# Rotary sums and the heads' high and low parts taken off DVE in the attention of an encoder trunk

## What is computed

```python
p = u @ w_in                                   # rq rk rv rg | dq dk dv
q = _rotary(rq, pos); k = _rotary(rk, pos) * 128 ** -0.5
# _rotary: concatenate([x1 * cos - x2 * sin, x1 * sin + x2 * cos])
ret = silu(rg) * groupnorm(retention(q, k, v)) # four heads "r"
a = softmax(q0 k0) - lam * softmax(q1 k1)      # four heads "d", q and k RMS-normed
dif = _rmsnorm(a @ v, subln_g) * (1.0 - lam_init)
h = h + jnp.concatenate([ret, dif], axis=-1) @ w_out
```

## Time and profile before

| | before |
|---|---|
| median of 3 runs | 1962.74 us (1961.9 to 1963.89) |
| the profiled execution, its own time | 1963.26 us |
| its span | 1960.6 us |
| PE busy | 1902.9 us (97%) |
| DVE busy | 1190.9 us (61%) |
| Pool busy | 1163.0 us (59%) |
| ACT busy | 915.5 us (47%) |
| granted PE clock, mean | 0.989 |

### The profile page before, as it was taken

How to read it: one execution, slowest core, us unless ns; L and a number is a source line. 1 busy time by engine, 2 the same in 40 slices (tenths; PEclk the granted TensorE clock), 3 DMA queues, 4 the chain that set the end, 5 groups by cost and what they waited for, 6 DMA issues and landing times.

```text
span 1960.6 us, 29609 instructions
## 1 busy us (share of the span) xinstructions
PE 1902.9 (97%) x11578; PEld 1692.3 (86%) x11578; DVE 1190.9 (61%) x1897; ACT 915.5 (47%) x1461; POOL 1163.0 (59%) x626
## 2 busy tenths in 40 slices
PE   7999999998899999999999999999988999999997
PEld 6989989886688998989879898998867889899896
DVE  7736667428665753736677376663385667457276
ACT  6534535446434643524565254454464355345254
POOL 4857757454243776857458585755533347588582
PEclk9999999999899999999999999999998999999999
DMA  3333423231122331332234233223211132323231
GB/s 130 133 108 109 137 94 108 75 107 55 54 65 72 111 130 65 108 108 88 85 105 143 77 109 108 87 87 118 87 54 54 54 108 87 118 92 115 86 104 69
DMA packets 54999, 186.46 MB, mean 95 GB/s; under 512 B 6441, under 2 KB 7977, under 8 KB 54861
## 3 DMA queue, kind: packets, MB, share of 16 engines
q1 hardware_dynamic: 53136, 181.61, 28.0%
q10 hardware_dynamic: 1724, 2.96, 0.5%
HBM read 182.44 MB, written 3.15 MB: 95 GB/s over the span
## 4 chain that ended last, share of the span: by engine, by line
PE 77%; DVE 8%; POOL 5%; ACT 4%; issue 3%; DMA 1%; DVEq 0%; ACTq 0%; POOLq 0%
PE bank L661 16%; PE bank L663 16%; PE bank L662 16%; PE pair L661 8%; PE pair L662 8%; PE pair L663 8%; POOL w_lo L573 1%; DVE neg_max L1737 1%; ACT s L1318 1%; PE pair L934 1%; PE bank L949 1%; DVE bank L1428 1%; DVE s L1724 1%; POOL w_lo_x L592 0%; POOL w_lo L592 0%
## 5 line engine op out<-in xcount | busy, mean ns | idle before, releaser
L565 POOL TENSOR_TENSOR w_lo<-raw,w_hi 128x1024 fp32r<-128x1024 f32 (+1 forms) x124 | 293.5, 2373 | 458.4 <-ACT w_hi L1016 458.4
L661 PE MATMUL bank<-hg_hi,w_hi 128*128 128x256 f32 (+1 forms) x1400 | 449.3, 321 | 2.3 <-DVE bank L1444 2.3
L663 PE MATMUL bank<-hg_hi,w_lo 128*128 128x256 f32 (+1 forms) x1400 | 444.6, 318 | 0.0
L662 PE MATMUL bank<-hg_lo,w_hi 128*128 128x256 f32 (+1 forms) x1400 | 444.2, 317 | 0.0
L661 PEld LDWEIGHTS bank<-hg_hi,w_hi 128*128 128x128 f32 x1400 | 265.5, 190 | 25.1 <-issue 7.9
L662 PEld LDWEIGHTS bank<-hg_lo,w_hi 128*128 128x128 f32 x1400 | 265.4, 190 | 18.2 <-issue 1.2
L663 PEld LDWEIGHTS bank<-hg_hi,w_lo 128*128 128x128 f32 x1400 | 265.3, 190 | 17.9
L1016 ACT ACTIVATE w_hi<-raw 128x1024 fp32r<-128x1024 f32 (+1 forms) x124 | 128.3, 1036 | 263.6 <-PE bank L663 127.8
L1411 DVE SCALAR_TENSOR_TENSOR h<-pair,h 128x512 f32<-128x512 f32 x100 | 68.9, 690 | 246.1 <-PE pair L663 245.8
L661 PE MATMUL pair<-a_hi,w_hi 128*128 128x512 f32 x440 | 172.5, 392 | 1.9 <-issue 1.3
L663 PE MATMUL pair<-a_hi,w_lo 128*128 128x512 f32 x440 | 171.6, 390 | 0.0
(11 more groups left out here) (269 smaller groups left out, 4951.9 us busy)
## 6 DMA issues: line engine op xcount, KB each, us to landing
raw<-in_w_gu SPq DMA_DIRECT2D x96, 512.0 KB, 3.7
raw_x<-in_w_gu SPq DMA_DIRECT2D x80, 512.0 KB, 4.1
raw<-in_w_p SPq DMA_DIRECT2D x56, 512.0 KB, 3.5
raw_x<-in_w_dn SPq DMA_DIRECT2D x32, 512.0 KB, 3.8
raw<-in_w_dn SPq DMA_DIRECT2D x32, 512.0 KB, 4.0
raw<-in_w_o SPq DMA_DIRECT2D x16, 512.0 KB, 3.5
raw_x<-in_w_dn SPq DMA_DIRECT2D x16, 384.0 KB, 3.6
raw<-in_w_dn SPq DMA_DIRECT2D x16, 384.0 KB, 3.4
```

The costliest lines, as they stand in the source:

```text
L565: pool.tensor_tensor(columns(lo_), raw_tiles(RAW_AT["e", e], TILES_OF[e]), columns(hi).bitcast(F32), ALU.subtract).then_inc(lo_done, 1)
L661: pe.matmul(out, hi[:, 0, :], m_hi, start=first, stop=False)
L662: pe.matmul(out, hi[:, 0, :], m_lo, start=False, stop=False)
L663: return pe.matmul(out, lo_[:, 0, :], m_hi, start=False, stop=last)
```

## The change

The rotary sum goes from DVE to Pool: `rotate` waits for `proj_free`, which DVE signals after its third multiplication, and stands ahead of `lo` in the same step. The high part of a finished head goes to ACT and its low part to Pool, both in the step after the one in which DVE finished the head, ahead of the rest of Pool's step and right behind `split` on ACT. Two semaphores are new: `head_done` (DVE to ACT) and `head_hi` (ACT to Pool). In ACT's step the square of a "d" head's output and its high part now come before the wait for `mix_ready`. The loops of ACT and Pool have one more step. PE's program is not changed.

```diff
--- before.py
+++ after.py
@@ -129,6 +129,7 @@
 
 STEPS = 31
 N_ITEMS = HEADS * BATCHES
+SUB_LATER = 1
 
 
 def scores_at(n): return 11 + n
@@ -166,7 +167,7 @@
 
 H_UPDATES = KD * (2 * len(CHUNKS) + 1)
 STATS = 1 + 8 + HEADS + HEADS + 1 + 1
-DVE_STEPS = 72
+DVE_STEPS = 56
 
 EARLY = 6
 FIRST_X = 3
@@ -380,6 +381,8 @@
         ret_sq = signal("ret_sq", HEADS)
         o_ret_free = signal("o_ret_free", HEADS)
         ret_rms = signal("ret_rms", HEADS)
+        head_done = signal("head_done", KD)
+        head_hi = signal("head_hi", KD)
         mix_ready = signal("mix_ready", KD)
         log_exp = signal("log_exp", 2)
         log_done = signal("log_done", 2)
@@ -631,13 +634,31 @@
                 pool.wait_ge(sq_hi, at(sq_hi, l, n + 1))
                 pool.tensor_tensor(lo_, squares, hi.bitcast(F32), ALU.subtract).then_inc(sq_lo, 1)
 
+            def rotate(l, t):
+
+                kind, hd = TILES[t]
+                dst = rkq[:, hd % 2, int(kind == "rq"), :]
+                pool.wait_ge(proj_free, at(proj_free, l, t + 1))
+                pool.tensor_tensor(dst, dst, s3[:, 0, :], ALU.add).then_inc(rot_ready, 1)
+
+            def lo_head(l, which, out):
+                k = MIX_ORDER.index(which)
+                pool.wait_ge(head_hi, at(head_hi, l, k + 1))
+                pool.tensor_tensor(a_lo[:, k, :], out, a_hi[:, k, :].bitcast(F32), ALU.subtract).then_inc(mix_ready, 1)
+
             def attention(l):
                 for t in range(AHEAD):
                     lo(l, E_ATT + t)
-                for t in range(STEPS):
+                for t in range(STEPS + 1):
+                    if (hd_n := at_step(subln_at, HEADS, t - SUB_LATER)) is not None:
+                        lo_head(l, ("d", hd_n), o_d[:, :])
+                    if (hd_n := at_step(ret_var_at, HEADS, t - 1)) is not None:
+                        lo_head(l, ("r", hd_n), o_r[:, :])
                     if t < PROJ_TILES:
+                        kind, hd = TILES[t]
+                        if kind in ("rk", "rq"):
+                            rotate(l, t)
                         lo(l, E_ATT + AHEAD + t)
-                        kind, hd = TILES[t]
                         if kind in ("dk", "dq"):
                             lo_square(l, "qk", 2 * hd + (kind == "dq"))
                     if (n := at_step(mixv_at, N_ITEMS, t)) is not None and n % 2:
@@ -1272,13 +1293,22 @@
                         act.wait_ge(decay_arg, at(decay_arg, l, i + 1))
                         act.activation(decay[:, i, :], decay[:, i, :], ACT.Exp).then_inc(decay_exp, 1)
 
+            def hi_head(l, which, out):
+                k = MIX_ORDER.index(which)
+                act.wait_ge(head_done, at(head_done, l, k + 1))
+                act.activation(a_hi[:, k, :], out, ACT.Copy).then_inc(head_hi, 1)
+
             def attention(l):
                 factor(l, stat_index("mix"), rms[:, :], 1.0, rms_ready)
-                for t in range(STEPS):
+                for t in range(STEPS + 1):
                     kind, hd = TILES[t] if t < PROJ_TILES else (None, 0)
                     if t < PROJ_TILES:
                         act.wait_ge(proj_done, at(proj_done, l, t + 1))
                         split(l, E_ATT + AHEAD + t)
+                    if (hd_n := at_step(subln_at, HEADS, t - SUB_LATER)) is not None:
+                        hi_head(l, ("d", hd_n), o_d[:, :])
+                    if (hd_n := at_step(ret_var_at, HEADS, t - 1)) is not None:
+                        hi_head(l, ("r", hd_n), o_r[:, :])
                     if kind == "rg":
                         act.wait_ge(proj_free, at(proj_free, l, t + 1))
                         act.activation(rg[:, hd, :], rg[:, hd, :], ACT.Silu).then_inc(rg_ready, 1)
@@ -1305,12 +1335,12 @@
                     if (n := at_step(mixv_at, N_ITEMS, t)) is not None and n % 2:
                         hd_n = n // 2
                         act.wait_ge(mixv_done, at(mixv_done, l, n + 1))
+                        act.activation(s3[:, 1, :], o_diff, ACT.Square).then_inc(o_d_sq, 1)
+                        hi_square(l, "sub", hd_n, o_d_sq)
                         if hd_n:
 
                             act.wait_ge(mix_ready, at(mix_ready, l, MIX_ORDER.index(("d", hd_n - 1)) + 1))
-                        act.activation(s3[:, 1, :], o_diff, ACT.Square).then_inc(o_d_sq, 1)
                         act.activation(o_d[:, :], o_diff, ACT.Copy).then_inc(o_d_ready, 1)
-                        hi_square(l, "sub", hd_n, o_d_sq)
                     if (n := at_step(scores_at, N_ITEMS, t)) is not None:
                         act.wait_ge(max_ready, at(max_ready, l, n + 1))
                         for i in range(2 * QT):
@@ -1687,14 +1717,6 @@
                                              op0=ALU.subtract, op1=ALU.subtract).then_inc(dve_step, 1)
                     next_step(l)
 
-            def mixed(l, which, source):
-
-                k = MIX_ORDER.index(which)
-                dve.tensor_copy(a_hi[:, k, :], source).then_inc(dve_step, 1)
-                dve.wait_ge(dve_step, next_step(l))
-                dve.tensor_tensor(a_lo[:, k, :], source, a_hi[:, k, :].bitcast(F32), ALU.subtract)\
-                    .then_inc(mix_ready, 1)
-
             def attention(l):
                 dve.wait_ge(rms_ready, at(rms_ready, l, 2))
                 dve.wait_ge(bias_in, at(bias_in, 0, 48))
@@ -1752,9 +1774,7 @@
                     if (hd_n := at_step(subln_at, HEADS, t)) is not None:
                         dve.wait_ge(sub_rms, at(sub_rms, l, hd_n + 1))
                         dve.scalar_tensor_tensor(out=o_d[:, :], in0=o_d[:, :], scalar=SUB_GAIN, in1=sub_factor,
-                                                 op0=ALU.mult, op1=ALU.mult).then_inc(dve_step, 1)
-                        dve.wait_ge(dve_step, next_step(l))
-                        mixed(l, ("d", hd_n), o_d[:, :])
+                                                 op0=ALU.mult, op1=ALU.mult).then_inc(head_done, 1)
                     if (hd_n := at_step(ret_var_at, HEADS, t)) is not None:
                         if hd_n:
                             dve.wait_ge(mix_ready, at(mix_ready, l, MIX_ORDER.index(("r", hd_n - 1)) + 1))
@@ -1764,9 +1784,7 @@
                         dve.wait_ge(o_ret_free, at(o_ret_free, l, hd_n + 1))
                         if hd_n == 0:
                             dve.wait_ge(rg_ready, at(rg_ready, l, HEADS))
-                        dve.tensor_tensor(o_r[:, :], o_r[:, :], rg[:, hd_n, :], ALU.mult).then_inc(dve_step, 1)
-                        dve.wait_ge(dve_step, next_step(l))
-                        mixed(l, ("r", hd_n), o_r[:, :])
+                        dve.tensor_tensor(o_r[:, :], o_r[:, :], rg[:, hd_n, :], ALU.mult).then_inc(head_done, 1)
 
             def take_over(l, t):
 
@@ -1784,8 +1802,6 @@
 
                     dve.tensor_tensor(cross[0:HALF], source[HALF:P], cs[HALF:P, 1, :], ALU.mult)
                     dve.tensor_tensor(cross[HALF:P], source[0:HALF], cs[0:HALF, 1, :], ALU.mult).then_inc(proj_free, 1)
-                    dve.wait_ge(proj_free, at(proj_free, l, t + 1))
-                    dve.tensor_tensor(dst, dst, cross, ALU.add).then_inc(rot_ready, 1)
                     return
                 if kind in ("dk", "dq"):
                     if hd == 3:
```

## The result

| | before | changed |
|---|---|---|
| median, runs on the same chip | 1962.6 us (10 runs, 1960.23 to 1963.89) | 1967.59 us (10 runs, 1966.61 to 1968.03) |
| ratio, 95% interval | | 1.0025 (1.0015 to 1.0035) |
| the profiled execution: own time, span | 1963.26, 1960.6 us | 1967.66, 1964.8 us |
| DVE busy, Pool busy | 1190.9, 1163.0 us | 1166.0, 1198.6 us |

The changed kernel is 5.0 us slower (by the interval 2.9 to 6.9). DVE lost 25 us of work and Pool gained 36 us, and PE, which bounds the kernel, came out later.

A forecast was written before the change was run, and what follows sets the result against it. PE, 97% busy, was taken to bound the kernel. Terms of 0.1 + 2.4 + 1.1 + 1.35 = 4.95 us a layer, 9.9 for both, on 1963.26 gave 1973.2, stated as 1972; range 1953 to 1977.

The forecast's parts named there:

- The mechanism: DVE's softmax port instructions each wait out a running Pool instruction; Pool instructions standing ready back to back decide the delay.
- the walk through step 17: Ahead of stall D: Pool's low part, rotary sum, weights and squares in turn; softmax ready at 507.5, as before.
- Stall E not longer: Rival, chance 0.22: L1719 precedes d1's low part or one of Pool's four is not ready; +2.9, 1965.6 us.
- Faster: Rival, chance 0.20: Pool does not get back to back into the softmax; 1943.5, or 1952.5 with E alone gone.
- Slower still: Rival, chance 0.08: Pool's squares of steps 24 and 26 are late too; up to +5.4 us, 1978.
- D: PE's transposes in step 18 (item 5) wait 3.01 us for DVE's softmax at 507.54; forecast +0.1 us a layer.
- E: PE's transposes in step 20 (item 7) wait 4.24 us for DVE's softmax at 529.45; forecast +2.4 us idle a layer.
- clock behind the stalls: PE's slow clock after a stall, taken as about half the idle; E's longer idle adds +1.1 us a layer.
- step 28: PE's statistic of "r" head 2 would newly wait for Pool's squares, ready at 593.55; +1.35 us a layer.

The follow-up runs named there:

- heads_only: The changed kernel with the rotary sum given back to DVE, so only the heads' parts moved: 1964.15 us, 1.0012 of the kernel before.
- late16: The changed kernel with Pool's weights of steps 16 to 19 made last, after the softmax: 1942.59 us, 0.9898 of the kernel before.
- ret_sq_first: The changed kernel with Pool's squares of the r heads ahead of the weights in steps 23, 25 and 27: 1965.26 us, 1.0015 of before.

## Why the prediction was right in direction and too large in size

**The mechanism held, step by step.** The count of Pool instructions ready in a row while DVE has its softmax to do decided both stalls, and the walk through step 17 came out within 0.3 us at each point: low part at 499.92 (forecast 500.0), weights 502.49 (502.6), squares done 506.14 (506.4), softmax ready 507.21 (507.5). *Stall E not longer* and *Faster* did not happen. Their margin did: DVE's `den` is recorded at 523.08, 0.04 us ahead of Pool's 523.12, and still waited. Of *Slower still* there is no sign: no such wait in steps 24 and 26.

**Terms of the sum, first layer.**

| term | forecast | measured |
|---|---|---|
| D, idle | +0.1 | -0.3 |
| E, idle | +2.4 | +1.8 |
| clock behind the stalls | +1.1 | -0.7 |
| step 28 | +1.35 | +1.28 |
| sum | 4.95 | 2.1; PE at step 28 is 2.08 later |

D and E are smaller mainly for one reason: I lengthened Pool's instructions by 0.15 to 0.3 us for each DVE instruction that passes between them. They were not: 1.29, 2.35, 1.31 and 2.39 us. The lengthened ones of the earlier trace rows, 1.47 at 527.64 and 2.53 at 529.07, had each let an L1724 instruction pass; those that let L1741 (was L1719) pass are not longer. Against that, Pool's low part began 0.4 us earlier than reckoned and caught `den`, which I had let pass; so five DVE instructions, not four, met the four of Pool, and the last two ended 0.68 us after it instead of one ending 0.28 after. E's stall begins at 525.04 (531.07 less 6.03) against 525.21, and ends 1.62 later; forecast were 2.5 with D's share.

**The step that failed is the clock term.** I took half of the idle as lost behind it, and so let 2.4 us more idle cost 1.1 us more. Here is the granted clock in pieces of 2 us behind E, first of the kernel before, then of the changed one:

```profile
526.00:528.00 2.00, 0.00 (x0) 0.00 (x0) 1.89 (x7) 2.00 (x4) 0.36 (x1) 0.83 0.80 246
...
532.00:534.00 2.00, 2.00 (x10) 1.94 (x9) 0.00 (x0) 0.60 (x1) 0.00 (x0) 0.50 0.70 197
534.00:536.00 2.00, 2.00 (x9) 1.61 (x9) 0.00 (x0) 1.92 (x3) 0.00 (x0) 0.96 0.16 66
```

```profile
526.00:528.00 2.00, 0.00 (x0) 0.00 (x0) 2.00 (x2) 0.59 (x1) 2.00 (x3) 0.81 0.20 31
...
532.00:534.00 2.00, 2.00 (x7) 1.65 (x7) 0.00 (x0) 0.01 (x1) 0.00 (x0) 0.50 0.52 197
534.00:536.00 2.00, 2.00 (x14) 1.79 (x14) 0.00 (x0) 1.63 (x3) 0.00 (x0) 0.99 0.00 0
```

The slow stretch (0.50, that is 1.2 GHz) begins near 527.3 in both and ends near 534.1 in both, some 6.8 us. It begins inside the idle. Before, PE came back at 529.45 and worked 4.6 us at half speed; after, it came back at 531.07 and worked 3 us so. The longer stall swallowed a part of the slow stretch instead of adding to it: it cost 0.8 us less, where the sum has 1.1 more. PE's own rows say the same: L906 starts 1.62 us later than before, the statistic behind it 1.06 later (534.68 against 533.62), and the one behind that (L760, L739 before) 0.81 later (534.99 against 534.18). Behind D the clock cost 0.1 more; together this is the -0.7 of the table.

In the second layer the sum does not come out as in the first, which the prediction had taken for granted: the layer cost 3.15 us up to step 28. PE of the kernel before, to lay beside the changed kernel's rows of this layer above:

```profile
1472.95 1.12 PE L885 MATMUL bank<-ident,s 128*128 128x128 f32 x4 [4.60 <-DVE s L1724]
...
1494.87 1.11 PE L885 MATMUL bank<-ident,s 128*128 128x128 f32 x4 [3.99 <-DVE s L1724]
...
1557.87 0.58 PE L738 MATMUL bank<-a_hi,ones_r 128*128 128x512 f32 x1
```

D's idle went from 4.60 to 2.68 and E's from 3.99 to 7.31 us. Yet the ends of D and E moved as in the first layer. From attention's first small wait (456.71 and 1422.15 before, 456.68 and 1423.40 changed) D ends after 50.8 us before and 50.6 changed, and E after 72.7 and 74.4, in both layers alike. So E ends 1.6 us later by the change in either layer, and what the clock does ahead of a stall only decides how much of the time up to its end PE spends idle. Behind the 3.1 us stall of step 16 of this layer the clock fell in the changed kernel and not in the one before:

```profile
1456.00:1458.00 2.00, 2.00 (x11) 1.65 (x10) 1.93 (x6) 0.00 (x0) 0.01 (x1) 1.00 0.46 119
```

```profile
1456.00:1458.00 2.00, 2.00 (x7) 1.54 (x6) 2.00 (x1) 0.45 (x1) 2.00 (x1) 0.50 0.00 0
```

That made PE 1.7 us later, and D's shorter idle gave it back. Only what follows E counts: there the longer stall cost 0.8 us less clock in the first layer and 0.2 more in the second (L906 is 2.89 later than L885, the product with v ten microseconds on 3.13), where the slow stretch lasted longer too, to 1503.4 against 1500.1 us. That is the difference between the layers: 1.6 - 0.8 + 1.3 = 2.1, and 1.6 + 0.2 + 1.3 = 3.1, the last term being step 28.

**Step 28** was the right wait at the right place and of nearly the right size. PE's scores in front of it start 0.80 us later than before (591.47 against 590.67) and the statistic 2.08 later: 1.28, forecast 1.35. The recorded idle of 0.93 is smaller because it counts from the modelled end of those scores, and the statistic of the kernel before starts 0.35 us ahead of that end (592.21 against 590.67 + 1.89). Pool's row ended 0.7 us later than forecast (594.24 against 593.55), but so did PE's work in front of it: ACT's copy that starts the row waits for PE. By the page of the Trainium skill named in the prediction (GPSIMD Engine Reference, section 3.1 Elementwise) each moved instruction would be an estimated 1.33 us (1.96 times DVE's 0.68 of the earlier trace rows); the rows of after have 1.27 to 1.30.

**What I left out:** between the layers PE won back 0.8 us of the 2.08: attention of the second layer begins 1.25 us late. PE is 2.0 us late up to 994 us, 1.6 behind its largest wait of that stretch (for DVE's L1476 before, L1506 after, which fell from 4.3 to 3.9 us) and 1.3 at 1086 us. Why it won back the part behind the wait I haven't located. So 2.08 - 0.8 + 3.15 = 4.4, of which the span shows 4.2.

## What to carry to other kernels

Before moving elementwise work from DVE to Pool, count the Pool instructions that will stand ready back to back while DVE does work that others wait for: each holds DVE's next instruction of the kinds seen here (two SBUF inputs, or `den` and the scaling behind it) until its end, and here the kernel came out 5 us slower although DVE had 25 us less to do. First make Pool's deferrable work wait for the end of DVE's urgent work; moving the weights of eight steps behind one semaphore wait took 32 us off the kernel before (1963.28 to 1931.11), six times what the change had cost. Don't price a clock fall as a share of the idle: see when it begins, what PE has to do in it, and whether a stall behind it takes the loss up again. And compare the layers: the same wait can have another clock in each.

## What the runs showed of the hardware

- How long DVE is held does not depend on how small its instruction is: `den` on 128x2 elements takes 0.23 us alone and 1.15 or 1.36 us beside a Pool instruction. What Pool loses to the DVE instruction that gets through between is nothing (1.29, 2.35), 0.2 us (1.47, 2.53) or 0.4 (1.72, squares behind the rotary sum in heads_only), by which instruction that is.
- The slow stretch of PE's clock (0.50) had the same start and the same end (527.3 to 534.1 us) for stalls of 4.2 and 6.0 us in the first layer. In the second it began near 1493.2 us in both kernels and ended at 1500.1 us for a stall of 4.0 and at 1503.4 for one of 7.3.
- The clock's fall in 490 to 494 us came in the kernel before and in the changed one behind a 3.1 us stall in step 16. late16 has the same stall (3.11 us, PE again busy at 488.88) and kept 1.00, as did heads_only and ret_sq_first. In the second layer the kernel before kept 1.00 behind it (3.09 us at 1454.16) and the changed one fell to 0.50 (3.11 us). What tells these apart is open.
